# A second mixer woven into one order: weight pieces between the small attention, retention and compression steps

## What is computed

```python
def hybrid_mixer(h, w_in, cmp_pe, cmp_w1, cmp_w2, nsa_out_g, ret_gn_g, w_out):
    parts = jnp.split(h @ w_in, IN_OFFSETS, axis=-1)
    q_n, kc, vc, ks, vs, kw, vw, gates, q_r, k_r, v_r, g_r = parts
    o_nsa = nsa_mixer(q_n, kc, vc, ks, vs, kw, vw, gates, cmp_pe, cmp_w1, cmp_w2)   # 8 heads of 64
    o_nsa = rms_norm_2(o_nsa, nsa_out_g)
    o_ret = retention(q_r, k_r, v_r, g_r, ret_gn_g)                                 # 4 heads of 128
    return jnp.concatenate([o_nsa, o_ret], axis=-1) @ w_out
```

## Time and profile before

| | |
|---|---|
| median of three runs | 3701.41 us |
| profiled execution, its own time | 3700.87 us |
| its span | 3699.1 us |
| PE busy | 3409.8 us (92%) |
| DVE busy | 2390.0 us (65%) |
| ACT busy | 1468.9 us (40%) |
| DMA, mean rate | 186 GB/s |
| chain that ended last: PE | 81% |

### The profile page before, as it was taken

The page is one execution under the profiler, slowest core; times in us unless marked ns, Lnnn a source line. Parts: engine busy times, 40 slices in busy tenths (PEclk is TensorE's granted clock), DMA queues, the critical chain, the costliest instruction groups (busy, mean ns, idle before and its releaser), DMA issues.

```text
span 3699.1 us, 58720 instructions
## 1 busy us (share of the span) xinstructions
PE 3409.8 (92%) x22220; PEld 3087.8 (83%) x22220; DVE 2390.0 (65%) x4104; ACT 1468.9 (40%) x1545; POOL 229.0 (6%) x48
## 2 busy tenths in 40 slices
PE   6879999999997989999999989996989899978898
PEld 2879899998873879899998879896889798867897
DVE  6757996556768658996557765464545455546454
ACT  1434454333321434454343333444443343444433
POOL 0005600000000007500000000000000000000000
PEclk9989999999998989999999999997999999979999
DMA  9414467666767324466666765542335455423353
GB/s 367 171 69 160 157 222 251 207 211 225 245 215 316 137 103 161 163 223 239 213 214 228 246 233 191 182 171 80 138 140 184 168 179 195 158 102 123 142 183 137
DMA packets 154052, 688.78 MB, mean 186 GB/s; under 512 B 10339, under 2 KB 76771, under 8 KB 78947
## 3 DMA queue, kind: packets, MB, share of 16 engines
q1 hardware_dynamic: 149264, 663.79, 50.4%
q10 hardware_dynamic: 4564, 22.21, 1.6%
HBM read 649.26 MB, written 36.70 MB: 185 GB/s over the span
## 4 chain that ended last, share of the span: by engine, by line
PE 81%; DVE 10%; ACT 3%; issue 2%; DVEq 1%; DMA 1%; PEld 1%; ACTq 0%; PEldq 0%
PE ps L685 25%; PE ps L923 19%; PE ps L691 13%; PE ps L718 9%; PE ps L725 4%; PE ps L902 3%; DMA work<-in_mem 1%; ACT work L1156 1%; PE ps L763 1%; PE ps L657 1%; DVE position_hot L1802 1%; DVE position_hot L1805 1%; DVE scr L1767 1%; DVE scr L1760 1%; PE ps L770 1%
## 5 line engine op out<-in xcount | busy, mean ns | idle before, releaser
L1164 ACT ACTIVATE weights_upper<-weights 128x2048 fp32r<-128x2048 f32 x520 | 996.1, 1917 | 1694.4 <-PE ps L685 950.3
L1495 DVE TENSOR_TENSOR weights_lower<-weights,weights_upper 128x2048 fp32r<-128x2048 f32 x476 | 1090.3, 2291 | 749.1 <-ACT weights_upper L1164 748.3
L685 PE MATMUL ps<-hT_upper,weights_upper 128*128 128x256 f32 x4416 | 626.1, 284 | 3.5 <-ACT hT_upper L1326 3.5
L685 PE MATMUL ps<-hT_lower,weights_upper 128*128 128x256 f32 x4416 | 625.0, 284 | 0.2
L691 PE MATMUL ps<-hT_upper,weights_lower 128*128 128x256 f32 x4416 | 575.3, 283 | 4.1 <-POOL weights_lower L622 4.1
L685 PEld LDWEIGHTS ps<-hT_upper,weights_upper 128*128 128x128 f32 x4416 | 571.9, 192 | 7.1 <-ACT hT_upper L1326 6.7
L685 PEld LDWEIGHTS ps<-hT_lower,weights_upper 128*128 128x128 f32 x4416 | 571.1, 192 | 4.6 <-issue 1.0
L691 PEld LDWEIGHTS ps<-hT_upper,weights_lower 128*128 128x128 f32 x4416 | 549.7, 192 | 5.0 <-POOL weights_lower L622 5.0
L622 POOL TENSOR_TENSOR weights_lower<-weights,weights_upper 128x2048 fp32r<-128x2048 f32 x44 | 228.8, 5214 | 1299.3 <-ACT weights_upper L1164 1299.3
L923 PE MATMUL ps<-weights_upper,hidden_lower 128*128 128x512 f32 x1024 | 253.5, 390 | 0.0
L923 PE MATMUL ps<-weights_upper,hidden_upper 128*128 128x512 f32 x1024 | 252.9, 389 | 0.0
(11 more groups left out here) (311 smaller groups left out, 3478.7 us busy)
## 6 DMA issues: line engine op xcount, KB each, us to landing
weights<-in_parts SPq DMA_DIRECT2D x264, 1024.0 KB, 4.8
weights<-in_experts SPq DMA_DIRECT2D x256, 1024.0 KB, 4.8
weights<-in_ada_w SPq DMA_DIRECT2D x24, 2048.0 KB, 11.3
scr<-gates SPq DMA_DIRECT2D x32, 1024.0 KB, 8.1
gates<-h SPq DMA_DIRECT2D x16, 1024.0 KB, 4.8
gates<-work SPq DMA_DIRECT2D x16, 1024.0 KB, 4.8
mod<-in_row ACTq DMA_DIRECT2D x3, 1536.0 KB, 6.2
rowp<-in_row ACTq DMA_DIRECT2D x2, 1550.0 KB, 19.6
```

Source lines behind the costliest of these rows:

```text
L685: m = mm(bank[:, e * T:(e + 1) * T], up[:, c, e * P:(e + 1) * P], s_[:, c, :], start=(e == 0 and n == 0 and c == 0), stop=False, skip_grou ...
L1164: f(upper[:, p_.r % SPLIT, :], raw[:, p_.r, :], ACT.Copy).then_inc(upper_ready, 1)
L1495: v.tensor_tensor(lower[:, s, :], raw[:, p_.r, :], upper[:, s, :].bitcast(F32), ALU.subtract)\
```

## The change

The plan, and with it the order of the weights in memory, is new: 6 `nin` (queries, compression, both key sets), 2 `nsv` (attention values and gates), 4 `ret` (retention queries and keys), 2 `rv`, 4 `cw1`, 2 `rg` (retention gates), 4 `nout`. There are 20 pieces ahead of `nout` before (10 + 6 + 4) and after (6 + 2 + 4 + 2 + 4 + 2), with the same matmuls in each. The two score sets get buffers of their own (`near`, `sel`), in which the transposed tiles overwrite the probabilities. The compression input is made by 8 additions and 2 large instructions. The retention result has a buffer `ro` of its own, and its root is taken by an own ACT instruction. PE's order is now

`nin` x6, `wS`, `nsv` x2, `lS`, `ret` x4, `rS`, `rv` x2, `wPT`, `rO`, `cw1` x4, `wO`, `hidT`, `lPT`, `kc`, `rg` first piece, `cS`, `lO`, `cPT`, `rg` second piece, `cO`, `oT`, `nout`.

The plan of the banks:

```diff
             p.fill("nT", 4)
-            p.fill("nin", 10, parts=1)
-            p.fill("nint", 6, parts=2)
+            p.fill("nin", 6, parts=1)
+            p.fill("wS", NSA_H)
+            p.fill("nsv", 2, parts=2)
+            p.fill("lS", NSA_H)
+            p.fill("ret", 4, parts=1)
+            p.fill("rS", RH)
+            p.fill("rv", 2, parts=2)
+            p.fill("wPT", NSA_H)
+            p.fill("rO", 2)
             p.fill("hid", 1, parts=4, of="cw1")
+            p.fill("wO", 2)
             p.fill("hidT", 1)
+            p.fill("lPT", NSA_H)
             p.fill("kc", 1)
+            p.fill("rg", 2, parts=2)
             p.fill("cS", 1)
-            p.fill("wS", NSA_H)
+            p.fill("lO", 2)
             p.fill("cPT", 1)
             p.fill("cO", 2)
-            p.fill("wPT", NSA_H)
-            p.fill("wO", 2)
-            p.fill("lS", NSA_H)
-            p.fill("rS", RH)
-            p.fill("lPT", NSA_H)
-            p.fill("lO", 2)
-            p.fill("rO", 2)
             p.fill("oT", 4)
```

PE, its first half (the steps that follow move in the same way, bodies unchanged):

```diff
+                pe.wait_ge(*k.emptied("nin", 5))
+                all_scores("wS", 2)
+                parts_by_token(k, l, "nsv", 0, 0, cols=280)
+                all_scores("lS", 0)
+                for i in range(4):
+                    parts_by_feature(k, l, "ret", i)
+                for i in range(4):
+                    pe.wait_ge(*k.emptied("ret", i))
+                for i in range(RH):
+                    pe.wait_ge(*k.free("rS", i))
...
+                parts_by_token(k, l, "rv", 0, 0)
+                all_turns("wPT", "wexp", near)
...
+                for t in range(TT):
+                    pe.wait_ge(*k.emptied("rv", t))
+                for i in range(RH):
+                    pe.wait_ge(*k.emptied("rS", i))
```

ACT:

```diff
+                ahead("nsv", 0, 2)
+                for t in range(TT):
+                    act.wait_ge(*k.filled("nsv", t))
+                    act.sem_inc(S("held"), 1)
+                    f(stat(152 + 24 * t, 24), k.bank("nsv", t)[:, 256:280], ACT.Sigmoid)
+                for t in range(TT):
+                    f(vt2[:, t, 0:256], k.bank("nsv", t)[:, 0:256], ACT.Copy).then_inc(k.empty_sem("nsv", t), 1)
+                softmax_exp(near, NSA_H, 40, 56, "wmax", l + 1, "wexp")
+                for i in range(2):
+                    ahead("ret", i)
+                    take(k, "ret", i, qr[:, 2 * i:2 * i + 2, :])
+                softmax_exp(sel, NSA_H, 88, 104, "lmax", l + 1, "lexp")
+                for i in range(2):
+                    ahead("ret", 2 + i)
+                    take(k, "ret", 2 + i, kr[:, 2 * i:2 * i + 2, :])
+                ahead("rv", 0, 2)
+                for i in range(NSA_H):
+                    take(k, "wPT", i, near[i], src=k.bank("wPT", i)[:, 0:384])
                 ahead("cw1", 0, 4)
                 act.wait_ge(*k.filled("hid"))
                 f(hidc[0:30, :], k.bank("hid")[0:30, :], ACT.Silu).then_inc(k.empty_sem("hid"), 1)
+                for i in range(NSA_H):
+                    take(k, "lPT", i, sel[i], src=k.bank("lPT", i)[:, 0:384])
+                ahead("rg", 0)
+                act.wait_ge(S("ret_inv_var"), l + 1)
+                f(stat(264, 8), stat(256, 8), ACT.Sqrt).then_inc(S("ret_rstd"), 1)
                 act.wait_ge(S("cmax"), l + 1)
                 f(cS[:, :], cS[:, :], ACT.Exp).then_inc(S("cexp"), 1)
...
+                ahead("rg", 1)
+                for t in range(TT):
+                    take(k, "rg", t, gr[:, t, :], ACT.Silu)
+                root("two", l + 1)
```

DVE (the `drain` between dependent instructions left out here; `maxima` and `combine` do what they did, `factor` is the old reciprocal and product; the steps `hidT`, `kc` and `cS` stand unchanged behind `combine("wO", 2)`):

```diff
+                ahead("nin", 4)
+                for s in range(2):
+                    for a_ in range(2):
+                        taps = Z[:, 2 * s:2 * s + 2, :].rearrange("p g (n j e) -> p g n j e", j=JP // 2, e=2)
+                        pe_ = colp[:, K2["pe"] + s * JP + a_ * JP // 2:][:, 0:JP // 2]
+                        for g_ in range(2):
+                            v.tensor_tensor(Zsum[:, s, a_ * JP // 2:(a_ + 1) * JP // 2, g_ * NCMP:(g_ + 1) * NCMP]
+                                            .rearrange("p j n -> p n j"), taps[:, g_, a_:a_ + NCMP, :, 0],
+                                            row(pe_, NCMP), ALU.add)
+                ahead("nin", 5)
+                v.tensor_copy(Zp2[0][:, :, :, :], Zsum)
+                v.tensor_tensor(Zp2[1][:, :, :, :], Zsum, Zp2[0][:, :, :, :].bitcast(F32), ALU.subtract)\
+                    .then_inc(S("zp"), 1)
+                maxima("wS", near, 24, "wmax")
+                ahead("nsv", 0, 2)
+                maxima("lS", sel, 72, "lmax")
+                ahead("ret", 0, 4)
+                for i in range(RH):
+                    v.wait_ge(*k.filled("rS", i))
+                    v.tensor_tensor(rS[i], k.bank("rS", i)[:, 0:384], retm[:, i, :], ALU.mult)\
+                        .then_inc(k.empty_sem("rS", i), 1)
+                ahead("rv", 0, 2)
+                for t in range(TT):
+                    take(k, "rv", t, vr[:, t, :])
+                factor(2, 56, "wexp")
+                factor(1, 104, "lexp")
+                for t in range(TT):
+                    v.wait_ge(*k.filled("rO", t))
+                    v.tensor_copy(ro[:, t, :], k.bank("rO", t)).then_inc(k.empty_sem("rO", t), 1)
+                for t in range(TT):
+                    v.tensor_reduce(stat(248 + 4 * t, 4), roh[t], AX.X, ALU.add)
+                ahead("cw1", 0)
+                v.tensor_scalar(stat(248, 8), stat(248, 8), 1.0 / P, None, ALU.mult)
+                for t in range(TT):
+                    v.tensor_tensor(roh[t], roh[t], column(stat(248 + 4 * t, 4), P), ALU.subtract)
+                ahead("cw1", 1)
...
+                ahead("cw1", 2)
...
+                ahead("cw1", 3)
+                v.tensor_scalar(stat(256, 8), stat(256, 8), 1.0 / P, EPS2, ALU.mult, ALU.add)
+                v.reciprocal(stat(256, 8), stat(256, 8)).then_inc(S("ret_inv_var"), 1)
+                combine("wO", 2)
                 v.wait_ge(*k.filled("hidT"))
...
+                combine("lO", 1)
+                v.wait_ge(S("ret_rstd"), l + 1)
+                for t in range(TT):
+                    v.tensor_tensor(roh[t], roh[t], column(stat(264 + 4 * t, 4), P), ALU.mult)
+                for t in range(TT):
+                    v.tensor_tensor(ro[:, t, :], ro[:, t, :], mod[:, R2["ret"]:R2["ret"] + 512], ALU.mult)
                 v.wait_ge(*k.filled("cPT"))
                 v.tensor_copy(cPT[:, :], k.bank("cPT")).then_inc(k.empty_sem("cPT"), 1)
+                ahead("rg", 0, 2)
+                for t in range(TT):
+                    v.wait_ge(*k.emptied("rg", t))
+                    v.tensor_tensor(h[:, t, 512:D], ro[:, t, :], gr[:, t, :], ALU.mult)
                 combine("cO", 0)
                 mean_squares([(onsa[:, t, :], tmpB[:, t, :]) for t in range(TT)], [512] * TT)
+                rstd("two", l + 1, EPS2)
```

More of the change, by code:

```diff
@@ L494, in two_mixers_and_peer_then_nsa_retention_memory @@
         vt2 = view(work, 7168, 560, "p (a n) -> p a n", a=TT)
-        sA = view(work, 8688, 3072, "p (h n) -> p h n", h=NSA_H)
-        PT = view(work, 11760, 3072, "p (h n) -> p h n", h=NSA_H)
+        near = [view(b, at_ + 384 * j, 384) for b, at_, n in ((h_all, 0, 5), (work, 9648, 3)) for j in range(n)]
+        sel = [view(b, at_ + 384 * j, 384) for b, at_, n in
+               ((work, 10800, 3), (work, 1024, 2), (scr, 3072, 2), (work, 14336, 1)) for j in range(n)]
+        ro = view(work, 3072, 1024, "p (a n) -> p a n", a=TT)
+        Zsum = view(scr, 2048, 960, "p (s j n) -> p s j n", s=2, j=JP)
         retm = view(work, 14832, RH * 384, "p (h n) -> p h n", h=RH)
@@ new lines, in all_turns, with all_values @@
+                def all_turns(name, exp_signal, src):
+                    pe.wait_ge(S(exp_signal), l + 1)
+                    for i in range(NSA_H):
+                        turn(k, name, i, src[i])
+                def all_values(name, turned, src, c0):
+                    pe.wait_ge(*k.free(name, 0))
+                    pe.wait_ge(*k.free(name, 1))
+                    for i in range(NSA_H):
+                        pe.wait_ge(*k.emptied(turned, i))
+                        c = c0 + (i // 4) * HD
+                        three_blocks(k.bank(name, 0)[:, i * HD:(i + 1) * HD], k.bank(name, 1)[:, i * HD:(i + 1) * HD],
+                                     src[i], vt2[:, 0, c:c + HD], vt2[:, 1, c:c + HD])
+                    pe.drain().then_inc(k.fill_sem(name, 0), 1)
+                    pe.drain().then_inc(k.fill_sem(name, 1), 1)
@@ L969, in _ @@
+                pe.drain().then_inc(k.fill_sem("rO", 0), 1)
+                pe.drain().then_inc(k.fill_sem("rO", 1), 1)
                 pe.wait_ge(S("zp"), l + 1)
@@ L987, in _ @@
                     one_pass(Zp2[0], lo, stop=(i % 2 == 1)).then_inc(parts_done, 1)
+                for t in range(TT):
+                    pe.wait_ge(*k.emptied("nsv", t))
+                all_values("wO", "wPT", near, 2 * HD)
                 pe.wait_ge(*k.free("hidT"))
@@ L994, in _ @@
```

(18 more changed lines are left out.)

199 lines of the change are left out of this document (79 added, 120 removed).

## The result

| | before | after |
|---|---|---|
| median | 3701.62 us (3700.87 to 3702.02, 4 runs) | 3651.38 us (3649.62 to 3653.49, 4 runs) |
| span of the profiled execution | 3699.1 us | 3650.1 us |
| ratio | | 0.9866, 95% interval 0.9854 to 0.9877 |

The change makes the kernel 50.2 us faster; 3648 were forecast. The page of the kernel after, engine rows as in the earlier trace rows: PE is busy 5.6 us less in 49.0 us less span, so most of what went was standing still.

The account below looks back on a forecast made before the run. It took PE, busy 92%, as bound, with time to win where mixer engines wait for each other. From 3700.87 us, layer gains 29.4 and 28.4 less 2 x 2.2 for clock made 53.4, so 3648; range 3636 to 3675.

Parts of the forecast that it names:

- the walk of the three queues: Mixer up to `lO`: stepping through PE, ACT and DVE, PE's end of `lO` comes near 101.4 us, against 131.0.
- PE's work: Up to `lO`: 56.6 us of pieces and 39.0 us of small steps, sum 95.6, nothing removed.
- My three idle stretches are 2.2, 1.1 and 1.8. A fall costs half of 3.2.: PE's clock: idle ahead of `nsv`, the last `lS` and `rS`; each fall costs 1.6 us, 1.4 falls assumed, 2.2 a layer.
- The waits: PE idle up to `lO`: 0.7 us at the start, 2.2 ahead of `nsv`, 1.1 at the last `lS`, 1.8 at `rS`.
- The tightest place of the walk: Fourth `cw1` piece: DVE's lower half ready at 72.3 us, wanted by PE at 72.6.
- `lO` and the tail: `lO` at DVE 102 to 104 us after the sixth `nin` piece, DVE's work to `oT` 18.3, `nout` at 124 to 126.
- The largest idle time of PE: Ahead of `oT`: about 10 us, ended by DVE.
- The first: From `nsv` on, 14 pieces arrive unconverted, 4.2 us each, 59 a layer: 3761 us; chance of slower 0.04.
- The second: PE's clock falls at some seven handovers from small to large steps, 11 us a layer: 3666; 3660 to 3675 shared 0.20.
- my three falls: PE's clock: upper bound of a fall at each idle stretch, ahead of `nsv`, the last `lS` and `rS`, 4.8 us.
- the third: PE dense, clock never lost, `kc` and `hidT` take 2 us, compression-input pair 0.69 each: 3639; below 3641 had chance 0.10.
- the fourth: A late-held bank keeps steps together; one knot with a softmax turn costs 12 us a layer: 3671; 3660 to 3675 shared 0.20.

Follow-up runs that it names:

- the combined kernel: Kernel after with `lO` ahead of `cS`, both `nsv` pieces ahead of `wS`, and lower halves of `nout` out of DVE's tail, all together: 3629.49 us.
- experiment 1: Kernel after with the weave undone: all 20 pieces first, then the small steps, `lPT` behind `kc` and `cS`: 3668.67 us.
- experiments 3: Kernel after with `lO` ahead of `cS` and the second `rg` piece ahead of `cPT`: 3646.09 us.
- 4: Kernel after with both `nsv` pieces ahead of `wS`, DVE's lower halves of the first two `ret` pieces moved along: 3643.52 us.
- experiment 6: Kernel after with the compression input made again by 64 small DVE instructions: 3666.33 us.
- 8: Kernel after with the lower halves of the first two `nout` pieces moved out of DVE's tail: 3646.12 us.
- experiments 2: Kernel after with 14 of the 16 calls of `cS` left out, 28 fewer matmuls per layer: 3632.22 us.

## Why the prediction was right, by its own steps

**Size and mechanism.** 53.4 us were forecast for the two mixers (29.4 + 28.4 - 4.4), and 52.4 came (25.8 + 26.6). The weaving moved the waits beside PE's pieces, as the walk of the three queues had it. But two errors met in the sum and nearly cancelled, so that it came out within 1 us is luck:

- *PE's work: 95.6 forecast, about 91.6 at full clock.* In the combined kernel it is 87.5 up to `lO` without `cS`, and `cS` is 4.1. The largest error was a row read at the wrong clock: the eight transposed tiles were priced at 4.9 by the earlier trace rows, where PE was near half clock (0.56, the row below, columns as in the earlier trace rows). After, 15 of their 24 matmuls take 1.86, some 0.12 each, so a set is about 3.0: 1.9 too much, twice. `hidT` and `kc` took PE 0.4 and 1.4 and not 3.0 in all; `cS` 4.0 and not 3.5.

```profile
2543.50:2548.40 4.90, 4.88 (x26) 4.88 (x27) 0.35 (x2) 3.19 (x7) 0.00 (x0) 0.56 0.00 0
```

- *The clock: 2.2 a layer forecast, 6.5 measured in layer 0 (98.1 busy less 91.6) and 4.6 in layer 1 (96.2 less 91.6).* The step that failed is "My three idle stretches are 2.2, 1.1 and 1.8. A fall costs half of 3.2." The idle stretch ahead of `nsv` did cost 1.8 in layer 0 (its first piece took 4.9 and not 3.06), though not in layer 1 after the same 2.12. The large fall, 4.6 in `lO`, came at no idle stretch.

Up to `lO` on DVE this makes 91.6 + 6.8 + 6.5 = 104.9 us in layer 0 and 91.6 + 6.8 + 4.6 = 103.0 in layer 1, where 95.6 + 5.8 + 2.2 = 103.6 was forecast.

**The waits.** Forecast 0.7, 2.2, 1.1, 1.8, in all 5.8; measured 0.69, 2.12, 0.71, 1.04, in all 4.6, each at its place and for its cause (ahead of `rS` the row names no releaser, but ACT's last take of `ret` ends at 2493.92, 0.1 us before PE goes on). One was missed: 1.22 ahead of the seventh `wPT` tile, whose bank DVE's take of `rv` empties. Together with gaps of 0.45 and 0.35 and smaller ones, 6.8 us. The copy of 960 columns took 0.66, its bound from below, the subtraction 1.16, as taken; the maxima began 0.3 us sooner than in the walk. The tightest place of the walk was the tightest: 0.3 us were forecast between the fourth `cw1` piece's lower half and PE's use of it, and 0.05 were left. The order of ACT's seven table loads, 1.28 each, is as told.

**`lO` and the tail.** `lO` was to reach DVE at t = 102 to 104; it came at 105.0 in layer 0 and 103.0 in layer 1. Then 18.4 and 18.8 to `oT` (18.3 forecast) and some 3.5 to `nout`, at 127.0 and 125.2 (124 to 126). The largest idle time of PE is ahead of `oT`, as forecast, with 8.59 instead of about 10; about 1.5 of that is the second `rg` piece, whose first two passes ran at the low clock (2.05 and 1.56 us, the next two 1.09).

**The rivals.** The first (pieces late, slower than before) is refuted: PE's timeline lists no wait ahead of any pass of `ret` or `cw1` for a half. The second was half true. The Trainium skill (TensorE: Matmul & The Clock Gate, "A second HAM failure mode: psum-queue depth-cycling") reports that repeated handovers with small idle times cost the clock in another kernel. The runs here don't bear that out for this kernel: the combined kernel has waits of 0.71, 1.03, 1.23, 0.45 and 0.35 us between its groups and a clock of 1.00 over all of them. Yet the clock was lost in a place that my three falls didn't name. Of the third, the low prices came (0.66 for the copy, 1.8 for `kc` and `hidT`), but not the dense PE that keeps its clock. Of the fourth, one bank was late, 1.22 us at the seventh `wPT` tile, but none held up a softmax turn.

**What carried the gain,** which the prediction did not separate: by medians, 33 of 50 us come with the order of the small steps, the two sets, the early retention norm and the shorter tail of experiment 1 (of these, 6.5 the two sets), and 17 with the weave. The new form of the compression input is no separate gain but a condition of the new order: without it the kernel after is 15 us slower, and in the kernel before it changes nothing. The early retention norm was not tried alone.

## What to carry to other kernels

When a serial stretch is woven into a stream of large pieces, walk every queue and read each duration at the clock at which it will run; a row from the idle stretch that is to vanish is too dear. What lay in an engine's slack before can stand on the path after, as 64 small DVE instructions did. And once PE is dense, the tail of the stage is what another engine does last: move work out of it together with whatever releases it, since here each move alone only showed the next wait.

## What the runs showed of the hardware

**A run of narrow matmuls costs the clock without any idle time.** 32 fp32 matmuls of 15 columns on 64 rows (`cS`, 3.98 us) follow PE's dense work at once; in layer 0 of the kernel after the granted clock is 1.2 GHz (0.50) half a microsecond behind them, and `lO` takes 10.1 us where it takes 5.4 at 2.4 GHz. With `cS` behind `lO` the fall is in `cS` (5.50 us); with 28 of the 32 left out it doesn't come. The same holds in both layers of every profiled execution in which the whole run follows dense work (kernel after twice, experiments 3, 4, 6, 8 and 9): the clock is 1.00 for 3 us ahead of the run and falls between 2 and 5 us after its start, 14 times of 14. Why just this run does it, its columns, its rows or its cadence of 0.12 us, was not taken apart.

**The same idle stretch, once with a fall and once without:** after 2.12 us the next 16 matmuls of `nsv` took 3.53 us in layer 0 and 2.31 in layer 1. It was so in all five profiled executions with this wait (kernel after twice, experiments 2, 3 and 8): a fall in layer 0, none in layer 1. After 3.53 us (experiment 1) the next 15 matmuls took 3.30 us in layer 0 and 1.86 in layer 1. After 8.47 us (experiment 6) it fell in both. What differs between the layers stays open.

**A rounding copy of 128 x 960 fp32 on DVE takes 0.66 us, a subtraction of the same size 1.16.**
